# Cross attention issued between the projections, a second up pair on the un-normed sum, and evictions issued after weight splits

## What is computed

```python
def layer_norm(x, g, b):
    mu = x.mean(-1, keepdims=True)
    var = jnp.square(x - mu).mean(-1, keepdims=True)
    return (x - mu) * lax.rsqrt(var + EPS) * g + b

x = layer_norm(ALPHA * x + hybrid_mixer(x, ...), ln1_g, ln1_b)
x = layer_norm(ALPHA * x + memory_cross_attention(x, mem, xa_wq, xa_wkv, xa_wo), ln2_g, ln2_b)
# conv_ffn: x @ w_up gives g and val (2816 columns each), a causal depthwise
# convolution of 3 taps on both, then
h = (jax.nn.gelu(g) * val) @ w_down
```

## Time and profile before

| | us |
|---|---|
| median of 3 runs (928.4 to 932.17) | 928.68 |
| profiled execution | 929.85 |
| its span in the profile | 927.7 |
| PE busy | 855.3 (92%) |
| DVE busy | 656.6 (71%) |
| ACT busy | 499.2 (54%) |

### The profile page before, as it was taken

How to read it: one execution, slowest core, us unless ns; L and a number is a source line. 1 busy time by engine, 2 the same in 40 slices (tenths; PEclk the granted TensorE clock), 3 DMA queues, 4 the chain that set the end, 5 groups by cost and what they waited for, 6 DMA issues and landing times.

```text
span 927.7 us, 16289 instructions
## 1 busy us (share of the span) xinstructions
PE 855.3 (92%) x6578; PEld 817.9 (88%) x6578; DVE 656.6 (71%) x1017; ACT 499.2 (54%) x714; POOL 6.2 (1%) x15
## 2 busy tenths in 40 slices
PE   4999998997697999999987999999997899999995
PEld 4889986896597999999976999898996899999995
DVE  4775677787579977787777696777787666655443
ACT  4645447454465766664346566787646444444450
POOL 0200000000000000000000000000000000000000
PEclk8999999999798999999996999999998799999997
DMA  9774565865043566668860576455565277765531
GB/s 322 199 237 136 167 197 181 244 206 169 18 136 114 160 185 186 191 191 293 287 216 23 158 221 217 131 165 174 165 215 167 71 247 236 229 217 167 183 105 46
DMA packets 145578, 166.40 MB, mean 179 GB/s; under 512 B 5488, under 2 KB 135536, under 8 KB 145504
## 3 DMA queue, kind: packets, MB, share of 16 engines
q1 hardware_dynamic: 143888, 162.82, 56.0%
q0 software_dynamic: 544, 1.49, 0.7%
q10 hardware_dynamic: 1072, 1.05, 0.3%
HBM read 164.10 MB, written 1.25 MB: 178 GB/s over the span
## 4 chain that ended last, share of the span: by engine, by line
PE 69%; DVE 9%; ACT 5%; issue 1%; DVEq 0%; ACTq 0%
PE ps L169 47%; PE ps L424 21%; DVE X L148 2%; DVE lor L148 2%; ACT hir L145 1%; ACT FA L145 1%; DVE FA L148 1%; DVE FA L156 1%; ACT INH L145 1%; PE ps L172 1%; ACT L145 1%; ACT X L145 0%; DVE INL L148 0%; ACT SQ L145 0%; DVE FA L152 0%
## 5 line engine op out<-in xcount | busy, mean ns | idle before, releaser
L148 DVE TENSOR_TENSOR lor<-raw,hir 128x1024 fp32r<-128x1024 f32 (+1 forms) x268 | 309.8, 1173 | 123.9 <-ACT hir L145 109.6
L169 PE MATMUL ps<-INH,hir 128*128 128x256 f32 (+1 forms) x1288 | 374.0, 290 | 19.5 <-DVE lor L148 17.0
L424 PE MATMUL ps<-INL,hir 128*128 128x256 f32 (+1 forms) x1288 | 368.9, 286 | 5.7 <-DVE INL L148 5.5
L169 PE MATMUL ps<-INH,lor 128*128 128x256 f32 (+1 forms) x1288 | 367.3, 285 | 0.0
L145 ACT ACTIVATE hir<-raw 128x1024 fp32r<-128x1024 f32 (+1 forms) x268 | 266.0, 1014 | 127.8 <-PE ps L424 121.5
L169 PEld LDWEIGHTS ps<-INH,hir 128*128 128x128 f32 x1288 | 249.8, 194 | 26.5 <-issue 12.3
L424 PEld LDWEIGHTS ps<-INL,hir 128*128 128x128 f32 x1288 | 249.0, 193 | 7.0 <-DVE INL L148 7.0
L169 PEld LDWEIGHTS ps<-INH,lor 128*128 128x128 f32 x1288 | 249.4, 194 | 1.1 <-issue 1.0
L169 PE MATMUL ps<-HIH,hir 128*128 128x256 f32 (+1 forms) x640 | 183.0, 286 | 0.2 <-DVE small L152 0.2
L424 PE MATMUL ps<-HIL,hir 128*128 128x256 f32 (+1 forms) x640 | 181.1, 283 | 0.0
L169 PE MATMUL ps<-HIH,lor 128*128 128x256 f32 (+1 forms) x640 | 181.1, 283 | 0.0
(11 more groups left out here) (139 smaller groups left out, 657.6 us busy)
## 6 DMA issues: line engine op xcount, KB each, us to landing
raw<-in_w_in SPq DMA_DIRECT2D x64, 512.0 KB, 4.4
raw<-in_mod_wT SPq DMA_DIRECT2D x48, 512.0 KB, 4.7
raw<-in_ffn_w_up SPq DMA_DIRECT2D x44, 512.0 KB, 4.5
raw<-in_w_ffn_in SPq DMA_DIRECT2D x44, 512.0 KB, 4.6
raw<-in_ffn_w_down SPq DMA_DIRECT2D x20, 512.0 KB, 4.8
raw<-in_w_ffn_out SPq DMA_DIRECT2D x20, 512.0 KB, 3.4
raw<-in_xa_wkv SPq DMA_DIRECT2D x16, 512.0 KB, 4.0
raw<-in_xa_wq SPq DMA_DIRECT2D x8, 512.0 KB, 4.8
```

What stands on the lines that cost most here:

```text
L148: return DV.do(lambda e: e.tensor_tensor(o, a, b, op), *w)
L169: return PE.do(lambda e: e.matmul(o, l, r, start=start, stop=stop, skip_group_check=True), *w, inc=inc)
L424: return PE.do(lambda e: e.matmul(o, *b, start=False, stop=stop, skip_group_check=True), inc=stop)
```

## The change

The interface of the generators gets finer (`linears_g` can yield after every input block, `steps_of` issues a number of them), and `late_g` can be given other pools and holds its banks until they are evicted (`held`). With that:

- xq 2 and xq 3 are begun before the evictions of the units ahead of them, so that the weights' splits stand ahead of the evictions in the queues of ACT and DVE.
- The steps of `xattn` are issued between parts of xq 2, xq 3 and of xo 0 and 1, which are computed as a pair. `oc` moves to blocks 9 to 16 of HIH and HIL. All four X updates stand near the end of it, two of them after the pair.
- The splits of X into x2 in the second norm: gain and bias of X go from DVE (tensor_scalar) to ACT (`on_act`).
- Up 1 and 12 become a second late pair, in the five banks that are left and freed; their evictions go to GA[2] and GB[2]. Up 2 is computed before up 1 and 12 are evicted.

```diff
-        for c in range(4):
+        add2(("xo", 0), A["xa_wo"], 0, ("xo", 1), A["xa_wo"], 256)
+        for c in (2, 3):
             add(("xo", c), A["xa_wo"], 256 * c, 8)
         for c in range(11):
-            if c == 0:
-                add2(("up", 0), A["ffn_w_up"], 0, ("up", 11), A["ffn_w_up"], 2816)
+            if c < 2:
+                add2(("up", c), A["ffn_w_up"], 256 * c, ("up", 11 + c), A["ffn_w_up"], 2816 + 256 * c)
                 continue
...
-        def linears_g(keys, kt, x, outs=None):
+        def linears_g(keys, kt, x, outs=None, fine=False):
...
+                    if fine and k < n - 1:
+                        yield
...
+        def steps_of(g, n):
+            for _ in range(n):
+                next(g)
...
-        def late_g(keys, x):
-            bs = [(lin.get(), att.get()) for _ in keys]
+        def late_g(keys, x, pools=None):
+            bs = []
+            for c in range(len(keys)):
+                bs.append([])
+                for p in pools[c] if pools else (lin, att):
+                    bs[c].append(p.get())
+                    bs[c][-1].held = True
...
-                b.free = [a]
+                b.free, b.held = [a], False
...
-                    if inp is not None:
+                    if inp is not None and not on_act:
                         x = ts(d[:, i, :], d[:, i, :], gcol(k + i), bcol(k + i), ALU.mult, ALU.add, a, t_vec, h)
                     else:
                         x = act(d[:, i, :], d[:, i, :], ACT.Identity, a, t_vec, scale=gcol(k + i), bias=bcol(k + i))
...
             for c in range(4):
-                b, t = linear((key, c), kt, inp)
+                b, t = pre[c] if c < len(pre) else linear((key, c), kt, inp)
...
-        for c in range(4):
-            u = two[c] if c < 2 else run(late_g([("xq", c)], xg))[0]
+        def q_out(c, u):
             tqc.append(normal(c, u, QC[:, 2 * c:2 * c + 2, :], t_rows, *ph))
-            if c in (1, 2):
-                x_update()
-        oc = Inp(INH, INL)
+        oc = Inp(HIH[:, 9:17, :], HIL[:, 9:17, :])
...
+        heads = xattn()
+        g = late_g([("xq", 2)], xg)
+        steps_of(g, 3)
+        q_out(0, two[0])
+        q_out(1, two[1])
+        steps_of(g, 2)
+        next(heads)
+        u = run(g)[0]
+        g = late_g([("xq", 3)], xg)
+        steps_of(g, 2)
+        q_out(2, u)
+        steps_of(g, 3)
+        next(heads)
+        u = run(g)[0]
         xg = Late(*(v[:, 0:8 * (T + 2)].rearrange("p (k t) -> p k t", t=T + 2) for v in (HIHF, HILF)), 2)
         xg.free = [PE.now()]
-        for i, _ in enumerate(xattn()):
-            if i in (3, 4):
-                x_update()
+        g = linears_g([("xo", 0), ("xo", 1)], 8, oc, fine=True)
+        next(heads)
+        q_out(3, u)
+        next(heads)
+        steps_of(g, 3)
+        next(heads)
+        x_update()
+        next(g)
+        next(heads)
+        x_update()
+        two = run(g)
+        x_update()
+        x_update()
...
-        two, rows = late_ln(late_g([("up", 0), ("up", 11)], xg), parts, ln2_start)
-        t_up = []
-        for u, dst in zip(two, (GA[1], GB[1])):
-            t_up.append(normal(len(t_up), u, dst, t_rows, *gfree[1]))
-            next(ln2[0], None)
+        units, rows = late_ln(late_g([("up", 0), ("up", 11)], xg), parts, ln2_start)
+        g = late_g([("up", 1), ("up", 12)], xg, [(lin, att), (att, att)])
+        steps_of(g, 2)
         for _ in ln2[0]:
             pass
+        steps_of(g, 3)
+        def up_out(c):
+            for i, dst in enumerate((GA[c + 1], GB[c + 1])):
+                t_up[c, i] = normal(2 * c + i, units[2 * c + i], dst, t_rows, *gfree[c + 1])
+        up_out(0)
...
         for c in range(11):
             s = c % NG
-            b, t = linear(("up", c), 8, x2) if c else (Bank(GA[1].rearrange("p b t -> p (b t)")), t_up[0])
+            if c == 1:
+                units += run(g)
+                hid.free = [PE.now()]
+                pre[2] = linear(("up", 2), 8, x2)
+                up_out(1)
+            b, t = (pre.get(c) or linear(("up", c), 8, x2)) if c > 1 else (Bank(GA[c + 1].rearrange("p b t -> p (b t)")), t_up[c, 0])
```

More of the change, by code:

```diff
@@ L1079, in apply, with apply_g @@
             return run(apply_g(*a, **kw))
-        def apply_g(bm, br, src, dst, gcol, bcol, inp, *w, dfree=None, square=None, ready=None):
+        def apply_g(bm, br, src, dst, gcol, bcol, inp, *w, dfree=None, square=None, ready=None, on_act=False):
             br, tr_ = br
@@ L1260, in ln2_start @@
         def ln2_start(rows):
-            ln2.append(apply_g(*rows, xs, xs, lambda k: V("ln2_g", k), lambda k: V("ln2_b", k), x2))
-            for _ in range(3):
-                next(ln2[0])
-        two, rows = late_ln(late_g([("up", 0), ("up", 11)], xg), parts, ln2_start)
-        hid.free = [PE.now()]
+            ln2.append(apply_g(*rows, xs, xs, lambda k: V("ln2_g", k), lambda k: V("ln2_b", k), x2, on_act=True))
+            steps_of(ln2[0], 3)
+        units, rows = late_ln(late_g([("up", 0), ("up", 11)], xg), parts, ln2_start)
         t_rows = [rows[0][1], rows[1][1]]
-        t_up = []
-        for u, dst in zip(two, (GA[1], GB[1])):
-            t_up.append(normal(len(t_up), u, dst, t_rows, *gfree[1]))
-            next(ln2[0], None)
+        g = late_g([("up", 1), ("up", 12)], xg, [(lin, att), (att, att)])
+        steps_of(g, 2)
         for _ in ln2[0]:
             pass
+        steps_of(g, 3)
+        t_up = {}
+        def up_out(c):
+            for i, dst in enumerate((GA[c + 1], GB[c + 1])):
+                t_up[c, i] = normal(2 * c + i, units[2 * c + i], dst, t_rows, *gfree[c + 1])
+        up_out(0)
+        pre = {}
         late = None
@@ L1289, in build @@
                 hid_put(*m)
[L1290 removed]
+            b, t = linear(("up", 11 + c), 8, x2) if c > 1 else (Bank(GB[c + 1].rearrange("p b t -> p (b t)")), t_up[c, 1])
             tc2 = conv2(GB[s], b.ap, 3, "ffn_conv_w", "ffn_conv_b", 44, 22 + 2 * c, t, *gfree[s])
             b.free = tc2
[L1293 to L1294 removed]
+            if c < 2:
+                gfree[c + 1] = [*tc, *tc2]
             late = (c, act(GA[s], GA[s], ACT.Gelu_apprx_tanh, *tc), tc2)
```

7 lines of the change are left out of this document (2 added, 5 removed).

## The result

| | us |
|---|---|
| changed kernel, median of 4 runs (944.82 to 948.95) | 947.88 |
| kernel before, beside it, median of 4 runs (928.4 to 932.17) | 929.5 |
| ratio, 95% interval | 1.0188 (1.0154 to 1.0222) |
| profiled execution of the changed kernel, and its span | 944.82, 942.9 |

A forecast was written before the change was run, and what follows sets the result against it. PE, busy 92% of the span, was taken as the bound, fed by DVE and ACT in program order. Part A +8.9 and part B +10.8 make +19.7 us on 929.85: 949.5, or 948.4 for the median; range 938 to 956.

The forecast's parts named there:

- head 3's scores wait: Cross attention: PE idles 5.15 us until the eviction of xq 3, late in DVE's queue, is done.
- output block 3 waits: Output projection: PE idles 6.85 us for xo 3's split, behind two X updates, the vectors and both residuals.
- part A: Cross attention and output projection, to the second norm's rows: +8.9 us, bounds +4.6 (no clock drop) to +9.5.
- R: Moment of the second norm's rows' matmuls: 286.11 us before, forecast 295.0.
- up 3's second half waits: Feed-forward: PE idles 7.8 us because up 3's second half is split last in line, at R + 50.2.
- part B: Second up pair, from R to the end of up 3: +10.8 us, or +8.5 at full clock.
- the walk: The prediction's step-by-step pass through the new order of PE, DVE and ACT with profiled prices; it gave +19.7 us.
- Rival 1: Interleaving works because DVE and ACT keep up: faster, 920 us; chance 0.08.
- Rival 2: The clock does not drop at the new idles: +13.1 us, 943; chance 0.13.
- Rival 3: X updates slip in before the xo stall, part A 0 or -1, total +10, 939.5 us; chance 0.08.
- Rival 4: Idles of 2.0 and 2.4 us drop the clock too, each up to 5.1 us: 954 to 956; chance 0.06.
- Rival 5: The change does nothing because the order of instructions stays; no chance of its own was given.

The follow-up runs named there:

- x_early: Changed kernel with the four X updates issued earlier, two behind xq 3's eviction and two ahead of head 3's transposes: 939.97 us, ratio 1.0109.
- a_only: Kernel before with only the change's new attention and output projection, feed-forward part as before: 935.98 us, ratio 1.0069.
- a_x: a_only with the X updates issued early, as in x_early: 929.19 us, ratio 0.9996.
- keep_clock: Changed kernel with unread matmuls in two PE waits, 36 ahead of head 3's scores and 48 ahead of output block 3: 945.6 us, ratio 1.0173.
- a_q3: a_only with query block 3 one head step earlier and all four X updates in one piece behind head 3's steps: 927.81 us, ratio 0.9979.
- b_only: Kernel before with only the second up pair and gain and bias of X on ACT, attention as before: 939.7 us, ratio 1.0112.

## Why the prediction was right

Predicted 948.4, measured 947.88; the ratio predicted, 1.021 (948.4 by 928.68), is inside the measured interval. By its steps:

| step | predicted | changed kernel |
|---|---|---|
| head 0's scores wait | 2.0 | 2.42 |
| head 1's transposes wait | 2.4 | 0.66 (2.23 in x_early) |
| head 3's scores wait | 5.15 | 5.14 |
| output block 2 waits | 1.4 | 1.80 |
| output block 3 waits | 6.85 | 6.43 |
| up 11 waits for its split | 1.75, hardly any with the clock's drop | 0.16 at the start of its matmuls of 258 columns |
| part A, R | +8.9 | +6.3 (87.55 less 81.22) |
| up 2 waits | 7.15, to R + 23.7 | 7.14, to R + 23.95 |
| up 13 starts | R + 33.9 | R + 34.4 |
| up 3's second half waits | 7.8, to R + 50.2 | 6.24, to R + 50.8 |
| part B | +10.8 | +11.1 |
| stretches at clock 0.50 | 4 | 6, three in A and three up to the end of up 3 |

**Right:** the mechanism of both parts, the place and releaser of each wait, and that nothing is won or lost behind them: B, cut 156 us behind up 3, has +11.1, as at up 3 itself (55.66 less 44.53).

**Off in size:** the clock's term of part A. I took 8 us at half clock behind head 3's wait. The trace has clock 0.50 from about 236.4 to 243.2, but PE was idle until 238.36, so it worked at half clock for 4.8 us and lost 2.4 us and not 4.1. I had read the length as counted from the moment PE resumes; in this trace the clock is down before that. On the clock of before (1.48 us are added to the times of this trace) block 3's split comes at 275.98, where the walk with its drop has 277.65. That is 1.7 of the 2.6 us by which this execution's A is below the walk. The other 0.9 us lie between block 3 and R, 16.46 us against 17.35: behind block 3's wait PE worked 2.9 us at half clock and lost 1.4, where the walk took 3 us. (The walk's own net of 0.2 us there is 3 less 2.55, so 0.45.)

The number of drops was off too. The walk took it that a wait of 2.3 us doesn't lower the clock, as in the kernel before; behind head 0's wait of 2.42 us it did fall, 1.1 us after PE had resumed:

```profile
214.79:215.90 1.11, 1.10 (x5) 1.01 (x6) 1.07 (x3) 0.26 (x1) 0.00 (x0) 1.00 0.64 227
215.90:219.30 3.40, 3.40 (x14) 3.09 (x14) 2.57 (x4) 2.88 (x4) 0.00 (x0) 0.50 0.45 131
```

It cost nothing, since PE then waited 0.66 us at head 1's transposes and not the 2.23 us of x_early, where the clock held there: the transposes started 16.04 us behind head 0's scores, and 16.01 in x_early. In all, A has 17.1 us at clock 0.50 in this execution. In a_only, with the same attention, it has 20.5, and A is +8.8. So the size of this term changes between executions of the same code, and "+8.9" was its upper end and not its middle.

That the median still agreed to 0.5 us is in part luck. The forecast for the profiled execution was 949.5 and it took 944.82, the lowest of its four. Of these 4.7 us, 2.6 are part A's, 2.3 lie outside the two cuts (1.5 before the first, 0.8 behind the last), where the code is the same, 0.2 outside the span, and part B gives 0.3 back.

In part B up 3's second half waited 6.24 us and not 7.8: its split came at R + 50.8, as forecast, but PE had reached it at R + 44.6 and not at R + 42.4.

**The place of the blame** was not quite right. The prediction wrote of xo 3's splits standing behind updates, vectors and residuals together. x_early shows that the updates alone carry the loss of part A; with them moved, and the residuals where they were, A is 80.65 against the 81.22 of before.

**The rivals.** Rival 1 (faster, 920) was to decide at xo 3's split by 266.7 and up 3's second split by R + 42.4. They came at 276.0 (on the clock of before) and R + 50.8, so it is refuted for the change as it is. The 6.2 us that attention was to win didn't show either: with the stall at xo mended (a_x) the time is that of before, not below it. Rival 2 (no drop of the clock, 943): the clock drops; with two of the waits filled, keep_clock gives 945.6. Rival 3 (updates slip in before the xo stall, 939.5) was wrong for the change, but it is just what x_early builds, at 939.97. Rival 4 (more drops, 954 to 956): the drops came, also behind the 2.42 us wait, but not their price. It would need A at 95 or more, the forecast's 90.1 and 5.1 for one more drop; A stayed at 87.5 to 90.1 in the executions with this attention. Rival 5 fell with the first trace.

In a_q3 the stretch from 231 to 241.2, half idle before, is full in good part (7.86 us busy of 10.2), and A is 1.6 us shorter:

```profile
231.00:241.20 10.20, 7.86 (x33) 6.38 (x33) 6.54 (x19) 4.93 (x16) 0.00 (x0) 0.83 0.16 53
```

The rule that the prediction weighed, in the Trainium skill, Perfetto Trace Analysis, section Optimization Strategy, says that performance may be improved by interleaving regimes whose most-contended engines differ. The runs agree in direction at best, with 0.2% for a_q3, and only once the order of the two feeding engines was rearranged; as the change did it, the interleaving of attention and projections lost 0.7% (a_only).

## What to carry to other kernels

Before interleaving two stages to fill one engine, list for the engines that feed it what now stands ahead of each operand's preparation: with queues in program order, work that nobody waits for yet (here four updates of 1.3 us each) can cost more than the idle time that was to be filled. When an idle gap is filled and another of the same size opens elsewhere, look for a chain over the other engines (here 54 of 79.6 us in a_q3); measure between two fixed instructions, not by the gaps. And moving operations to the less busy engine pays only if the two don't then wait for each other in each step (3.7 us here).

## What was unexpected in the hardware's behaviour

At head 3 and at output block 3 TensorE's granted clock fell to 0.50 while the engine still waited, and was back 4.8 us after it resumed at head 3, and some 2.9 us after it resumed at output block 3. At head 0 it fell only after the engine had resumed, and stayed down for 3.4 us. In the kernel before, both stretches at 0.50 were 10.2 us long; here those two were about 6.8 us behind similar waits. In b_only, with the attention of before, the stretch at head 0's transposes was 6.8 us behind a wait of 7.65 us (7.70 and 10.2 before), and a wait of 2.54 us was followed by 3.4 us at 0.50, where the 2.53 us of before had none. So the price of a wait can't be read off its length. Waits of 7.14 and 6.24 us in part B fell together with clocks of 0.77 (306 to 316 us) and 0.68 (336 to 346.62 us):

```profile
306.00:316.00 10.00, 2.86 (x20) 2.65 (x20) 7.12 (x12) 4.95 (x8) 0.00 (x0) 0.77 0.21 65
...
336.00:346.62 10.62, 4.87 (x26) 4.90 (x27) 10.16 (x18) 6.75 (x10) 0.00 (x0) 0.68 0.32 96
```

The same program's executions differ with this: keep_clock took 941.28 and 942.34 us at a mean granted clock of 0.962 and 0.960, and 949.51 and 948.87 at 0.951 and 0.949. A difference of 2 us between two such kernels is therefore hard to tell from a few times, and one trace of each is no surer, as A of the same attention moved by 2.5 us: set the stretches side by side with their granted clock, and compare them with those of other kernels that share the code.
